# State sums of the S5 stage: from VectorE to GpSimd, in a hybrid decoder step on one core

## The chip, the core and the metric

The kernel runs on one core of one Trainium2 chip. The core has a matrix engine (TensorE, PE in the rows; its weight loads are PEld), a vector engine (VectorE, DVE), a scalar engine (ScalarE, ACT), GpSimd (POOL) and SyncE (SP, which issues most transfers here). They share an on-chip memory, SBUF; matrix products land in PSUM, called ps in the rows. Each engine runs its own list of instructions in order, and semaphores make one engine wait for another. The metric is the device time of one execution in microseconds (us), lower is better.

## What is computed

One inference step of a two-layer decoder, for a prompt of 256 positions and for 8 sequences with 4 new tokens each. Layer 0 is attention and gated linear attention, layer 1 an S5 state-space layer; a squared-ReLU channel mixer and a per-layer embedding follow each. The change lies in the S5 layer:

```python
    # 64 groups, one complex 64-dim state per group, u is the normed input
    bur = jnp.einsum('blgc,gpc->lbgp', u, bbr)
    bui = jnp.einsum('blgc,gpc->lbgp', u, bbi)
    ...
    _, _, xr, xi = lax.associative_scan(s5_combine, (ar, ai, bur, bui), axis=0)   # x[t] = lambda x[t-1] + bu[t]
    y = einsum(xr, c_re) - einsum(xi, c_im)      # y = Re(C x)
    y = y + d * n;  g = gelu(y);  zg = g @ w_glu
```

## The kernel before

The prompt is cut into 64 steps of four tokens, and the recurrence runs over the steps. The state indices lie on the 128 partitions in 32 blocks; the stage takes them in eight rounds of four blocks, numbered i from 0 to 7. A complex recurrence is made real by turning: the inputs v are multiplied by the cosines and sines of the angle of lambda to the power of the step (`rcos`, `rsin`), a real first-order scan with the magnitude (`mag`) runs over the steps, and its result is turned back by the same angles into the states X. The parts of a round are small functions in the list of VectorE:

- `turned_inputs(i)` (L2540, L2541): four products of the inputs, read from PSUM, with `rcos` and `rsin`, 128x256 each.
- `turning_back(i)` (L2562): two products of 128x512, from the scan's result `zs` into `pq` (two tiles in `sq`, used by every round).
- `turned_sums(i)` (L2547, L2548): a sum and a difference of 128x256 that finish the turned inputs.
- `states(i)` (L2568, L2569): a difference and a sum of 128x252 (four blocks of 63 steps) from `pq` into X. The second raises the semaphore `turned_back`.
- `scanned(i)` (L2556): two scans of 128x256, real and imaginary. Ahead of them VectorE waits for `x_start`, which the second of the turned sums raises.
- `normed_inputs(i + 3)` (L2528): one product that empties a PSUM bank of inputs for a later round.

VectorE's loop runs over nine rounds: `turned_inputs(i)`, `turning_back(i - 1)`, `turned_sums(i)`, `states(i - 1)`, `scanned(i)`, `normed_inputs(i + 3)`. The ninth has only `turning_back(7)` and `states(7)`. Behind the loop come `lo_half` (L2594, 128x1024) and `n_lo` (L1971, 128x288), which make the low parts of the first weights and inputs of the gated projection w_glu; its first half needs `lo_half(0, 0)` and four `n_lo`, the other four `n_lo` wait for ScalarE.

TensorE in each round makes the inputs of round i + 3 (L1427, L1363) and then `outputs(i)`: eight products with a Toeplitz matrix (L1435), in rounds 5 to 7 three products that only keep it busy (L1405), then a wait for `turned_back` at i + 1, and 16 products of X with C (L1443, L1444). Behind `outputs(7)` the products of the gated projection (L883 to L885) begin. ScalarE copies last states, applies GELU to the outputs (L1880) and makes the high parts of weights.

GpSimd makes `rcos`, `rsin` and `mag` ahead of the stage (tensor operations recorded at the helper's line L786), issues one transfer (L821), and then waits for `states_ready`, which VectorE raises after the stage, to issue two transfers of final states and one of the next embedding (L823 to L825).

Of the kernel before, what the change touches and what calls it, by code (L numbers as in the profile page):

```python
# [16 lines left out]
ALU = mybir.AluOpType  # L17
# [22 lines left out]
JP = TP // TS  # L40
# [235 lines left out]
def program(nc, ins, outs):  # L276
    g = plan()
    ctx = ExitStack()
    with ctx:
# [5 lines left out]
        with ExitStack() as names:  # L285
            inside, used = ([("a2hi", FB * T)] + [(f"hi{i}", UNIT) for i in range(HI[3])] + [("nhi", DB * T), ("phi", 2 * T), ("up1_lo", DB * T)]), S5A["Bre"][0]
            assert used == 0
            used = sum(size for _, size in inside)
            inside += [("between", S5A["a2"][0] - used), ("a2lo", FB * T)]
            assert inside[-2][1] > 0  # L290
            split = {n: names.enter_context(nc.sbuf_tensor(f"{n}_split", [P, size], F32R)) for n, size in shared[:-1] + inside}
        with ExitStack() as names:
            inside = [("before", sum(size for _, size in shared[:-1]) + AB["temp"][0])] + [(f"in_hi{i}", UNIT) for i in range(HI[0])] + [("in_nhi", DB * T)]
            assert HI[0] * UNIT <= AB["temp"][1]
            for n, size in inside:
                split[n] = names.enter_context(nc.sbuf_tensor(f"{n}_split", [P, size], F32R))
        with ExitStack() as names:

            inside = [("to_c", sum(size for _, size in shared[:-1]) + S5A["Cre"][0])] + [(f"up_hi{i}", UNIT) for i in range(HI[1])] + [("up_nhi", DB * T), ("up_lo", DB * T)]
            used = S5A["Cre"][0] + HI[1] * UNIT + 2 * DB * T  # L300
            assert used <= S5A["toep"][0]
            inside += [("to_a2", S5A["a2"][0] - used)] + [(f"a2{part}{half}", HALF) for half in range(2) for part in ("hi", "lo")]
            assert 4 * HALF == FB * T and UNIT <= HALF
            for n, size in inside:
                split[n] = names.enter_context(nc.sbuf_tensor(f"{n}_split", [P, size], F32R))
# [32 lines left out]
        def view(buf, offset, size, **shape):  # L338
            v = buf[:, offset:offset + size]
            if shape:  # L340
                keys = list(shape)
                v = v.rearrange("p (" + " ".join(keys) + ") -> p " + " ".join(keys), **{k: shape[k] for k in keys})
            return v
# [167 lines left out]
        to = a20 + SB * J  # L511
# [7 lines left out]
        X = view(arena, b0, 2 * SB * 128, r=2, s=SB, j=128)  # L519
# [7 lines left out]
        pq = [view(sq, 512 * i, 512, r=2, s=4, j=JP) for i in range(2)]  # L527
# [96 lines left out]
        def blocks_of(i, j=None):  # L624

            at = 16 * (i // 4) + i % 4
            return slice(at, at + 13, 4) if j is None else slice(at + 8 * j, at + 8 * j + 5, 4)
# [65 lines left out]
        def _(pool):  # L693
# [125 lines left out]
            pool.memset(mag[:, :, 0:1], 0.0).then_inc(rotation_ready, 1)  # L819
            pool.wait_ge(main_ready, g.of[("proj", 0, 7)][2])  # L820
            pool.dma_start(pT[:, 0:512], ins["x0"]).then_inc(x0_in, 16)  # L821
            pool.wait_ge(states_ready, 1)
            pool.dma_start(outs["s5_p"], arena[:, fin0:fin0 + 64]).then_inc(out_done, 16)  # L823
            pool.dma_start(outs["s5_s"], arena[:, vs0:vs0 + 512]).then_inc(out_done, 16)
# [1116 lines left out]
        def _(dve):  # L1941
            step = [0]
            V = nc.vector
# [581 lines left out]
            def normed_inputs(i):  # L2525

                ps = result(dve, ("u", i))
                V.tensor_tensor(ustk[:, blocks_of(i)], ps[:, 0:4 * J].rearrange("p (b j) -> p b j", j=J), bc(rsi.unsqueeze(1), [P, 4, J]),  # L2528
                                ALU.mult).then_inc(bank_of(("u", i)), 1)

            def turned_inputs(i):

                if i:
                    dve.wait_ge(scan_ready, 2 * i)
                for j in range(2):
                    name = ("v5", 2 * i + j)
                    ps = result(dve, name)
                    two = slice(2 * j, 2 * j + 2)
                    v = ps[:, 0:4 * J].rearrange("p (s r j) -> p r s j", s=2, r=2)[:, :, :, 0:JP]
                    V.tensor_tensor(z[:, :, two], v, bc(rcos[:, blocks_of(i, j)].unsqueeze(1), [P, 2, 2, JP]), ALU.mult).then_inc(bank_of(name), 1)  # L2540
                    V.tensor_tensor(zt[:, :, two], v, bc(rsin[:, blocks_of(i, j)].unsqueeze(1), [P, 2, 2, JP]), ALU.mult).then_inc(bank_of(name), 1)  # L2541

            def turned_sums(i):

                for j in range(2):
                    copied(dve, ("v5", 2 * i + j))
                V.tensor_tensor(z[:, 0], z[:, 0], zt[:, 1], ALU.add).then_inc(x_start, 1)  # L2547
                V.tensor_tensor(z[:, 1], z[:, 1], zt[:, 0], ALU.subtract).then_inc(x_start, 1)  # L2548

            def scanned(i):  # L2550

                if i >= 2:
                    dve.wait_ge(wfin_ready, i - 1)
                dve.wait_ge(x_start, 2 * i + 2)
                for r in range(2):
                    V.tensor_tensor_scan(flat(zs[i % 2][:, r]), flat(mag[:, 4 * i:4 * i + 4]), flat(z[:, r]), 0.0, ALU.mult, ALU.add).then_inc(scan_ready, 1)  # L2556

            def turning_back(i):

                dve.wait_ge(scan_ready, 2 * i + 2)  # L2560
                for x, rot in zip(pq, (rcos, rsin)):
                    V.tensor_tensor(x, zs[i % 2], bc(rot[:, blocks_of(i)].unsqueeze(1), [P, 2, 4, JP]), ALU.mult).then_inc(pow_done, 1)  # L2562

            def states(i):

                dve.wait_ge(pow_done, 2 * i + 2)
                to = X[:, :, blocks_of(i), 1:JP]
                V.tensor_tensor(to[:, 0], pq[0][:, 0, :, 0:JP - 1], pq[1][:, 1, :, 0:JP - 1], ALU.subtract).then_inc(x_ready, 1)  # L2568
                V.tensor_tensor(to[:, 1], pq[0][:, 1, :, 0:JP - 1], pq[1][:, 0, :, 0:JP - 1], ALU.add).then_inc(turned_back, 1)  # L2569

            copied(dve, ("ss", 3))
            for i in range(3):
# [2 lines left out]
            for i in range(9):  # L2575
                if i < 8:
                    turned_inputs(i)
                if i:
                    turning_back(i - 1)
                if i < 8:  # L2580
                    turned_sums(i)
                if i:
                    states(i - 1)
                if i < 8:
                    scanned(i)
                if i + 3 < 8:
                    normed_inputs(i + 3)
# [225 lines left out]
```

## Time and profile before

| | us |
|---|---|
| median of 3 runs | 987.06 (984.12 to 991.71) |
| the profiled execution's own time | 988.64 |
| its span, first to last instruction | 987.0 |
| TensorE busy (share of the span) | 943.7 (96%) |
| VectorE busy | 631.8 (64%) |
| ScalarE busy | 473.6 (48%) |
| GpSimd busy | 127.6 (13%) |

The profile is of one execution. Busy time is the union of an engine's instructions; a row of a timeline gives the start, the duration, the engine, the line, the operation and its tiles (out<-in), and in square brackets how long the engine sat idle before and what released it. Consecutive instructions of one line stand in one row with their number (x2). VectorE's next instruction often starts a little before the last one ends, so the distance of starts is what an instruction costs its queue. The S5 loop lies between 642 and 690 us of the span.

### The profile page before, as it was taken

Reading aid. Unit: us, or ns where it says so; the run is one execution under the profiler, and the core shown is the slowest. Engines: PE = TensorE matmul, PEld = TensorE weight load, DVE = VectorE, ACT = ScalarE, POOL = GpSimd, SP = SyncE. Lnnn points to the kernel's source line nnn. Section 1 sums busy time; section 2 is a strip of 40 time slices with the busy share of each in tenths; the row PEclk is TensorE's granted clock in tenths of the full one; section 3 lists DMA queues with packets and bytes.
Section 4 is the critical chain, followed back from the end, with each engine's and each line's share of the span. In section 5 each row is a group of like instructions: output and inputs, shape, how many; then the busy total and the mean of one; then the engine's idle time right before and its main releaser. Section 6 shows DMA issues by size and latency. Waiting matters only on the chain.

```text
span 987.0 us, 17733 instructions
## 1 busy us (share of the span) xinstructions
PE 943.7 (96%) x6831; PEld 868.3 (88%) x6831; DVE 631.8 (64%) x1118; ACT 473.6 (48%) x834; POOL 127.6 (13%) x215
## 2 busy tenths in 40 slices
PE   6999999989999799999999979999999999999997
PEld 6998478779888489999999967778999999999997
DVE  5653897788687258975586564399766666443453
ACT  6433565554334145755343546336665655433353
POOL 3420141000013220000000318800000000000000
PEclk9999999999879899999999999999999999999999
DMA  8580033211327653444444420500444444444431
GB/s 321 199 313 22 22 93 85 87 53 55 107 92 209 252 188 136 171 171 171 160 155 160 167 86 1 208 18 1 153 171 159 158 157 168 165 154 153 155 143 48
DMA packets 34773, 135.42 MB, mean 137 GB/s; under 512 B 5273, under 2 KB 17817, under 8 KB 22146
## 3 DMA queue, kind: packets, MB, share of 16 engines
q1 hardware_dynamic: 28802, 117.76, 33.3%
q0 software_dynamic: 5888, 16.53, 4.9%
q8 instruction: 54, 0.88, 0.4%
q14 instruction: 29, 0.24, 0.1%
HBM read 130.11 MB, written 4.17 MB: 136 GB/s over the span
## 4 chain that ended last, share of the span: by engine, by line
PE 77%; DVE 13%; ACT 3%; issue 3%; DMA 3%; SPq 1%; DVEq 0%; ACTq 0%; POOLq 0%
PE ps L883 18%; PE ps L884 17%; PE ps L885 17%; PE ps L915 4%; PE ps L1088 2%; PE ps L1090 2%; PE ps L1089 2%; DMA ring<-in_stream 2%; DVE arena L2411 1%; PE ps L1011 1%; PE ps L1427 1%; PE ps L1204 1%; DVE arena L2156 1%; DVE const L2556 1%; DVE arena L2152 1%
## 5 line engine op out<-in xcount | busy, mean ns | idle before, releaser
L885 PE MATMUL ps<-a2hi_split,ring_split 128*128 128x288 f32 x512 | 150.5, 294 | 0.0
L885 PEld LDWEIGHTS ps<-a2hi_split,ring_split 128*128 128x128 f32 x512 | 96.4, 188 | 0.0
L883 PE MATMUL ps<-nhi_split,hi_split 128*128 128x288 f32 x320 | 95.1, 297 | 0.1
L885 PE MATMUL ps<-nhi_split,ring_split 128*128 128x288 f32 x320 | 94.1, 294 | 0.0
L1967 DVE TENSOR_TENSOR ring_split<-ring,hi_split 128x2048 fp32r<-128x2048 f32 x36 | 82.2, 2285 | 17.5 <-ACT hi_split L1539 17.5
L1539 ACT ACTIVATE hi_split<-ring 128x2048 fp32r<-128x2048 f32 x36 | 68.7, 1910 | 31.4 <-PE ps L885 22.7
L1088 PE MATMUL ps<-sq_split,hT_split 128*128 128x288 f32 (+1 forms) x256 | 80.1, 313 | 3.6 <-DVE pages_lo_split L2134 3.3
L883 PE MATMUL ps<-up_nhi_split,up_hi_split 128*128 128x288 f32 x256 | 76.2, 298 | 0.9 <-DVE arena L2350 0.9
L1089 PE MATMUL ps<-wuk_lo_split,hT_split 128*128 128x288 f32 (+1 forms) x256 | 76.6, 299 | 0.0
L1090 PE MATMUL ps<-sq_split,pages_lo_split 128*128 128x288 f32 (+1 forms) x256 | 76.5, 299 | 0.0
L1539 ACT ACTIVATE up_hi_split<-ring 128x2048 fp32r<-128x2048 f32 x28 | 53.6, 1913 | 46.5 <-PE ps L885 44.8
L883 PE MATMUL ps<-a2hi_split,hi_split 128*128 128x288 f32 x256 | 75.8, 296 | 0.0
L884 PE MATMUL ps<-up_lo_split,hi_split 128*128 128x288 f32 x256 | 75.5, 295 | 0.0
L884 PE MATMUL ps<-up_lo_split,up_hi_split 128*128 128x288 f32 x256 | 75.5, 295 | 0.0
L884 PE MATMUL ps<-a2lo_split,hi_split 128*128 128x288 f32 x256 | 75.5, 295 | 0.0
L885 PE MATMUL ps<-up_nhi_split,ring_split 128*128 128x288 f32 x256 | 75.3, 294 | 0.0
L1967 DVE TENSOR_TENSOR ring_split<-ring,up_hi_split 128x2048 fp32r<-128x2048 f32 x28 | 63.9, 2284 | 11.7 <-ACT up_hi_split L1539 11.7
L915 PE MATMUL ps<-nT,ring 128*128 128x288 f32 x256 | 64.3, 407 | 0.0
L883 PEld LDWEIGHTS ps<-nhi_split,hi_split 128*128 128x128 f32 x320 | 60.0, 187 | 0.4 <-issue 0.3
L885 PEld LDWEIGHTS ps<-nhi_split,ring_split 128*128 128x128 f32 x320 | 60.2, 188 | 0.0
L915 PEld LDWEIGHTS ps<-nT,ring 128*128 128x128 f32 x256 | 48.3, 190 | 13.5 <-issue 0.4
L1088 PEld LDWEIGHTS ps<-sq_split,hT_split 128*128 128x128 f32 x256 | 51.2, 200 | 6.7 <-DVE pages_lo_split L2134 3.5
(426 smaller groups left out, 2597.5 us busy)
## 6 DMA issues: line engine op xcount, KB each, us to landing
ring<-in_stream SPq DMA_DIRECT2D x96, 1024.0 KB, 4.8
arena<-in_ckvT SPq DMA_DIRECT2D x64, 128.0 KB, 2.1
arena<-in_ckv POOLq DMA_DIRECT2D x23, 128.0 KB, 3.1
ring<-in_ckv POOLq DMA_DIRECT2D x21, 128.0 KB, 2.4
arena<-in_ckv SPq DMA_DIRECT2D x20, 128.0 KB, 2.8
arena<-in_wu POOLq DMA_DIRECT2D x1, 2240.0 KB, 10.2
arena<-in_s POOLq DMA_DIRECT2D x4, 512.0 KB, 3.5
out_gla_s<-arena POOLq DMA_DIRECT2D x4, 512.0 KB, 2.9
```

The costliest lines, as they stand in the source:

```text
L883: pe.matmul(ps[:, 0:T], wh[:, k, col:col + P], xh, start=first and k == which[0], stop=False)
L884: pe.matmul(ps[:, 0:T], wh[:, k, col:col + P], xl, start=False, stop=False)
L885: mm = pe.matmul(ps[:, 0:T], wl[:, k, col:col + P], xh, start=False, stop=last and k == which[-1])
L915: mm = pe.matmul(ps[base:base + m, 0:T], wv[:, k, col:col + m], rhs(k), start=first and k == which[0], stop=last and k == which[-1])
L1011: mm = pe.matmul(ps[0:NOPE, 0:T], wuk[:, k, key_columns(h):key_columns(h) + NOPE], ckvn[:, k], start=k == 0, stop=k == KB - 1)
L1088: pe.matmul(out, hi, wuk_hi[:, k, cols], start=start, stop=False, skip_group_check=True)
L1089: pe.matmul(out, hi, wuk_lo[:, k, cols], start=False, stop=False, skip_group_check=True)
L1090: return pe.matmul(out, lo, wuk_hi[:, k, cols], start=False, stop=stop, skip_group_check=True)
L1204: pe.matmul(ps[:, lo:lo + TS], s0[h % 2][:, b], qb[:, h, lo:lo + TS], start=False, stop=False, skip_group_check=True)
L1427: mm = pe.matmul(ps[:, (2 * n + r) * J:(2 * n + r) * J + J], bm[:, blk].rearrange("p i c -> p (i c)"), ustk[:, blk], start=n == 0 and r == ...
L1539: act.activation(hi_part(v)[:, :], ring[SPLITS[v] % RING][:, :], ACT.Copy).then_inc(hi_ready, 1)
L1967: V.tensor_tensor(lo_parts[slot][:, :], ring[slot][:, :], as_whole(hi_part(v)[:, :]), ALU.subtract).then_inc(unit_split, 1)
```

## The change

`states(i)` leaves VectorE's list and goes to GpSimd's, behind the transfer at L821 (the same lines are L827 and L828 in the kernel after, whose later lines are numbered 10 higher or, behind the loop, 4 higher). GpSimd waits for both products of `turning_back(i)`, then makes the difference and the sum. As `pq` is used by every round, `turning_back(i)` on VectorE now waits until the sums of round i - 1 are done.

```diff
@@ -819,6 +819,16 @@
             pool.memset(mag[:, :, 0:1], 0.0).then_inc(rotation_ready, 1)
             pool.wait_ge(main_ready, g.of[("proj", 0, 7)][2])
             pool.dma_start(pT[:, 0:512], ins["x0"]).then_inc(x0_in, 16)
+
+            def states(i):
+
+                pool.wait_ge(pow_done, 2 * i + 2)
+                to = X[:, :, blocks_of(i), 1:JP]
+                pool.tensor_tensor(to[:, 0], pq[0][:, 0, :, 0:JP - 1], pq[1][:, 1, :, 0:JP - 1], ALU.subtract).then_inc(x_ready, 1)
+                pool.tensor_tensor(to[:, 1], pq[0][:, 1, :, 0:JP - 1], pq[1][:, 0, :, 0:JP - 1], ALU.add).then_inc(turned_back, 1)
+
+            for i in range(8):
+                states(i)
             pool.wait_ge(states_ready, 1)
             pool.dma_start(outs["s5_p"], arena[:, fin0:fin0 + 64]).then_inc(out_done, 16)
             pool.dma_start(outs["s5_s"], arena[:, vs0:vs0 + 512]).then_inc(out_done, 16)
@@ -2557,16 +2567,12 @@
 
             def turning_back(i):
 
+                if i:
+                    dve.wait_ge(x_ready, i)
+                    dve.wait_ge(turned_back, i)
                 dve.wait_ge(scan_ready, 2 * i + 2)
                 for x, rot in zip(pq, (rcos, rsin)):
                     V.tensor_tensor(x, zs[i % 2], bc(rot[:, blocks_of(i)].unsqueeze(1), [P, 2, 4, JP]), ALU.mult).then_inc(pow_done, 1)
-
-            def states(i):
-
-                dve.wait_ge(pow_done, 2 * i + 2)
-                to = X[:, :, blocks_of(i), 1:JP]
-                V.tensor_tensor(to[:, 0], pq[0][:, 0, :, 0:JP - 1], pq[1][:, 1, :, 0:JP - 1], ALU.subtract).then_inc(x_ready, 1)
-                V.tensor_tensor(to[:, 1], pq[0][:, 1, :, 0:JP - 1], pq[1][:, 0, :, 0:JP - 1], ALU.add).then_inc(turned_back, 1)
 
             copied(dve, ("ss", 3))
             for i in range(3):
@@ -2579,8 +2585,6 @@
                     turning_back(i - 1)
                 if i < 8:
                     turned_sums(i)
-                if i:
-                    states(i - 1)
                 if i < 8:
                     scanned(i)
                 if i + 3 < 8:
```

On VectorE, one round of the loop before, from the last of the turned inputs to the next round's normed inputs (const, tmp, sq and arena are SBUF, ps is PSUM):

```order
L2541 TENSOR_TENSOR tmp<-ps,arena 128x2x128
L2562 TENSOR_TENSOR sq<-const,arena 128x512 x2
L2547 TENSOR_TENSOR const<-const,tmp 128x256
L2548 TENSOR_TENSOR const<-const,tmp 128x256
L2568 TENSOR_TENSOR arena<-sq 128x4x63
L2569 TENSOR_TENSOR arena<-sq 128x4x63
L2556 SCALAR_TENSOR_TENSOR const<-arena,const 128x256 x2
L2528 TENSOR_TENSOR arena<-ps,rs 128x4x72
```

The same place now:

```order
L2551 TENSOR_TENSOR tmp<-ps,arena 128x2x128
L2575 TENSOR_TENSOR sq<-const,arena 128x512 x2
L2557 TENSOR_TENSOR const<-const,tmp 128x256
L2558 TENSOR_TENSOR const<-const,tmp 128x256
L2566 SCALAR_TENSOR_TENSOR const<-arena,const 128x256 x2
L2538 TENSOR_TENSOR arena<-ps,rs 128x4x72
```

The two sums are gone, and the scans stand right behind the turned sums whose end they wait for.

On VectorE at the end of the loop before, from the last scans to the low parts of the gated projection:

```order
L2556 SCALAR_TENSOR_TENSOR const<-arena,const 128x256 x2
L2562 TENSOR_TENSOR sq<-const,arena 128x512 x2
L2568 TENSOR_TENSOR arena<-sq 128x4x63
L2569 TENSOR_TENSOR arena<-sq 128x4x63
L2594 TENSOR_TENSOR ring_split<-ring,glu_hi_split 128x1024
L1971 TENSOR_TENSOR nT_split<-nT,glu_nhi_split 128x288 x4
```

The same place now:

```order
L2566 SCALAR_TENSOR_TENSOR const<-arena,const 128x256 x2
L2575 TENSOR_TENSOR sq<-const,arena 128x512 x2
L2598 TENSOR_TENSOR ring_split<-ring,glu_hi_split 128x1024
L1981 TENSOR_TENSOR nT_split<-nT,glu_nhi_split 128x288 x4
L2598 TENSOR_TENSOR ring_split<-ring,glu_hi_split 128x1024
```

The low parts follow the last products of turning back at once; the last states are GpSimd's, at the same time.

## Rows read from the trace of the kernel before

**Rows 1.** Chain that ended last, in the S5 loop: start, us, what.
```profile
650.92 0.41 DVE arena L2569
...
682.82 0.42 DVE arena L2569
```

**Rows 2.** Busy time by stretch: us, busy of each engine, granted clock, DMA.
```profile
650.00:660.00 10.00, 8.41 (x79) 7.26 (x79) 10.00 (x26) 4.06 (x13) 0.00 (x0) 1.00 0.00 0
690.00:700.00 10.00, 10.00 (x77) 10.00 (x76) 7.91 (x13) 8.91 (x13) 0.00 (x0) 1.00 0.30 103
```

**Rows 3.** Timeline of VectorE, one round of the loop: start us, us, engine, line.
```profile
664.89 1.28 DVE L2562 TENSOR_TENSOR sq<-const,arena 128x512 f32<-128x512 f32 x2
666.10 0.42 DVE L2547 TENSOR_TENSOR const<-const,tmp 128x256 f32<-128x256 f32 x1
666.43 0.42 DVE L2548 TENSOR_TENSOR const<-const,tmp 128x256 f32<-128x256 f32 x1
666.77 0.41 DVE L2568 TENSOR_TENSOR arena<-sq 128x252 f32<-128x252 f32 x1
667.10 0.41 DVE L2569 TENSOR_TENSOR arena<-sq 128x252 f32<-128x252 f32 x1
667.43 1.26 DVE L2556 TENSOR_TENSOR_SCAN const<-arena,const 128x256 f32<-128x256 f32 x2
668.61 0.43 DVE L2528 TENSOR_TENSOR arena<-ps,rs 128x288 f32<-128x288 f32 x1
668.96 0.41 DVE L2540 TENSOR_TENSOR const<-ps,arena 128x256 f32<-128x256 f32 x1
```

**Rows 4.** Timeline of VectorE in round 0, where no sums of states stand between.
```profile
645.40 0.42 DVE L2548 TENSOR_TENSOR const<-const,tmp 128x256 f32<-128x256 f32 x1
645.86 1.27 DVE L2556 TENSOR_TENSOR_SCAN const<-arena,const 128x256 f32<-128x256 f32 x2
```

**Rows 5.** Timeline of GpSimd ahead of the loop, single operations on SBUF.
```profile
609.70 0.97 POOL L786 TENSOR_TENSOR arena<-arena 128x256 f32<-128x256 f32 x1
...
611.46 0.63 POOL L786 TENSOR_TENSOR arena<-arena 128x256 f32<-128x256 f32 x1
...
612.17 0.74 POOL L786 TENSOR_TENSOR arena<-arena 128x256 f32<-128x256 f32 x1
...
618.45 1.06 POOL L786 TENSOR_TENSOR arena<-arena 128x512 f32<-128x512 f32 x1
...
620.72 1.27 POOL L786 TENSOR_TENSOR arena<-arena 128x512 f32<-128x512 f32 x1
```

**Rows 6.** Timeline of VectorE at the same times.
```profile
609.64 0.46 DVE L2383 TENSOR_TENSOR hT<-hT,tmp 128x288 f32<-128x288 f32 x1
...
618.66 0.46 DVE L2378 TENSOR_TENSOR tmp<-ps,rs 128x288 f32<-128x288 f32 x1 [3.09 <-PE ps L915]
...
621.14 1.18 DVE L2383 TENSOR_TENSOR hT<-hT,tmp 128x288 f32<-128x288 f32 x1
```

**Rows 7.** Timeline of VectorE at the loop's end.
```profile
684.45 1.29 DVE L2562 TENSOR_TENSOR sq<-const,arena 128x512 f32<-128x512 f32 x2
...
686.12 0.41 DVE L2569 TENSOR_TENSOR arena<-sq 128x252 f32<-128x252 f32 x1
686.45 1.22 DVE L2594 TENSOR_TENSOR ring_split<-ring,glu_hi_split 128x1024 fp32r<-128x1024 f32 x1
687.58 1.56 DVE L1971 TENSOR_TENSOR nT_split<-nT,glu_nhi_split 128x288 fp32r<-128x288 f32 x4
689.06 1.22 DVE L2594 TENSOR_TENSOR ring_split<-ring,glu_hi_split 128x1024 fp32r<-128x1024 f32 x1
```

**Rows 8.** Timeline of TensorE at the loop's end, outputs of rounds 6 and 7.
```profile
683.38 0.41 PE L1443 MATMUL ps<-arena 128*128 128x71 f32 x2 [0.79 <-DVE arena L2569]
...
686.09 1.67 PE L1405 MATMUL ps<-hT,const 128*128 128x288 f32 x6
687.59 0.34 PE L1443 MATMUL ps<-arena 128*128 128x71 f32 x2
```

## Prediction

> **What bounds the kernel now.** I read the shares of busy time first: TensorE 96% of the span. A stage off TensorE can therefore matter only where TensorE waits for it. The chain that ended last shows one such place: between 650.92 and 683.24 us it runs through VectorE [rows 1], with the second state sum of each round in it. The busy time by stretch agrees: from 650 to 660 VectorE is busy for 10.00 of 10 us and TensorE for 8.41, at a granted clock of 1.00; from 690 on TensorE is busy for 10.00 of 10 again [rows 2]. So the S5 loop is VectorE's, what follows is TensorE's, and a shift of the loop's last outputs passes to the end of the kernel one for one. The timeline of VectorE then gives the round: products of turning back at 664.89, turned sums at 666.10 and 666.43, state sums at 666.77 and 667.10, scans at 667.43, normed inputs at 668.61, turned inputs from 668.96 [rows 3].
>
> **What is taken from VectorE.** The two sums cost its queue 667.43 - 666.77 = 0.66 us a round [rows 3]. Not all of it comes back. The scans wait for the end of the turned sums; before, the state sums lay in that wait. In round 0, where none lie there, the scan starts 0.46 after the second turned sum (645.40 to 645.86) [rows 4], against a distance of 0.33 between the two turned sums [rows 3]. That is 0.13 of new wait. The saving is 0.66 - 0.13 = 0.53 us a round.
>
> **What GpSimd pays.** Its row nearest in size is 128x256, 0.63 us for one kind and 0.74 for the one that writes in pieces [rows 5]; the sums also write in pieces (four of 63), so I take 0.74. Bounds: 0.6, and 1.0 since no row has this four-dimensional form. Between two such operations lie 612.17 - 611.46 - 0.63 = 0.08 us [rows 5]. A pair alone is 0.74 + 0.08 + 0.74 = 1.56 us. From the products' end to the next products VectorE has some 4 us of other work, so the new wait ahead of `turning_back` should cost nothing: its cover is the turned sums, scans, normed and turned inputs. Without that cover the pair would cost 1.56 x 7 = 11 us. GpSimd has nothing queued behind the sums but three transfers that wait for the end of the stage anyway.
>
> **What the two engines do to each other.** Here the trace speaks against the change. VectorE's hT<-hT,tmp takes 0.46 us at 609.64, but 1.18 at 621.14, where a GpSimd operation runs from 620.72 to 621.99 [rows 5, 6]. It was held for 0.72 and so began in earnest at 621.86, 0.13 before GpSimd's end. The other way round, GpSimd's operation at 609.70 started 0.06 after VectorE's and took 0.97 instead of 0.74 [rows 5, 6]: it was held for 0.23, that is until 609.93, 0.29 after VectorE's start. An operation of VectorE that reads PSUM and one SBUF tile (tmp<-ps,rs at 618.66) takes 0.46 beside a GpSimd operation that takes a plain 1.06 [rows 5, 6]. So where VectorE reads two SBUF tiles and GpSimd reads SBUF, one waits for most of the other; with an operand in PSUM it doesn't. In the loop, the turned sums, the scans and the products of turning back have two SBUF inputs, as the low parts behind it do; turned and normed inputs read PSUM.
>
> The Trainium skill says this as a rule (page "SBUF — State Buffer", section "Who interferes with whom"): a VectorE instruction with two SBUF inputs and a GpSimd instruction that reads SBUF exclude each other for the whole instruction, and the one that starts first goes first. The rows agree on who is held, but the hold is 0.29 of VectorE's 0.46 and all but 0.13 of GpSimd's. With whole instructions, the two delays worked out below would each be 0.13 longer, 0.26 x 7 = 1.8 us more in all. Without the rule the sum would be that of the second rival.
>
> Now one round, with time 0 where the first turned sum starts. The products end at 0.07 (664.89 + 1.28 against 666.10) [rows 3]; TensorE follows a VectorE semaphore after 0.14 (683.24 to 683.38) [rows 1, 8], so GpSimd's difference asks at 0.21. The turned sum holds the port for 0.29 x 256 / 288 = 0.26. If GpSimd gets in there, it holds from 0.26 to 0.87 (0.74 - 0.13 = 0.61), and the second turned sum, due at 0.33, waits **0.54**. It runs from 0.87 and lets go at 1.13; GpSimd's sum, ready at 0.87 + 0.13 + 0.08 = 1.08, holds from 1.13 to 1.74. The scan, due 0.46 after the second turned sum at 1.33, waits **0.41**. The states are done at 1.87. Delay 0.95, saving 0.53: **a round is 0.42 us longer**. Seven rounds of sums (0 to 6) lie ahead of the last products: +2.9 us.
>
> **The loop's end.** Before, the last products let go of the queue at 684.45 + 1.21 = 685.66 [rows 3, 7]; now at 688.6. There `lo_half` of 1024 columns follows at once [rows 7], holding the port for 0.29 x 1024 / 288 = 1.03. GpSimd's last difference waits for it, holds from 1.03 to 1.64, one `n_lo` of 288 columns slips in until 1.93, the sum holds until 2.54 and ends at 2.67, and TensorE's last outputs start 0.14 later: 688.6 + 2.8 = 691.4. Before, they start at 687.59 [rows 8]. That is **+3.8 us**. TensorE's fillers in front (686.09 [rows 8]) are then done; the low parts of the gated projection are ready by then or shift with the outputs.
>
> The profiled execution took 988.64 (span 987.0 and 1.6 around it), so the sum gives 988.64 + 3.8 = 992.4. This execution lies 1.58 above the median of the three runs, 987.06; for a median I forecast 987.06 + 3.8 = **990.9 us**.
>
> **Rivals.**
> (1) GpSimd doesn't get in between two pipelined VectorE operations, only where VectorE pauses or reads PSUM. No row shows two such operations in a row beside a waiting GpSimd one. Then the difference gets in at 0.59, ahead of the scan's wait, and delays it to 1.20 instead of 0.79 (0.41); the sum waits until the scans are over. A round is 0.53 - 0.41 = 0.12 shorter, seven give -0.8. But at the end it waits for `lo_half`, four `n_lo` and `lo_half` again: 689.06 - 686.45 + 1.03 = 3.64 [rows 7], then 1.56 and 0.14: 684.8 + 5.34 = 690.1, or +2.6 on TensorE: 989.7.
> (2) The other side: GpSimd runs beside VectorE (the scans, which no row shows beside GpSimd, don't use the port, or the sums seldom meet it). VectorE gains 0.53 x 7 = 3.7. TensorE gains less: its outputs of round 7 follow those of round 6 by its own work (683.38 to 687.59 [rows 8]), and those of round 6 come 6 x 0.53 = 3.2 earlier less 0.36, as states would be done 0.14 + 1.56 = 1.70 after the products' end against 667.51 - 666.17 = 1.34 now [rows 3]. So -2.8: 984.3. It decides once the two delays are below 0.53 a round. Held operations at 609.70 and 621.14 speak against it.
> (3) Slower by over 1%: GpSimd's operations are much longer in this form. Sixteen of them (14 delays, two at the end) pass their extra time on, so another 6.1 us on top of 3.8 needs 0.38 each, 1.12 instead of 0.74; at 1.0 the result is +8.0. Nothing in the rows of 256 columns comes near it unheld.
>
> **How the numbers follow.** Forecast 0.50, rival 1 0.20, rival 2 0.17, rival 3 0.05; 0.08 for cases between (0.6 us an operation gives 3.8 - 16 x 0.14 = +1.6; 1.0 gives +8.0). A run of this kernel can't tell less than about 1% (9.9 us) from no change, and the three runs differ by 7.6. The range goes from 984.0, which takes in half of rival 2, to 994.5, which takes in operations of 0.97 us and leaves rival 3 out; what is left out is 0.08 + 0.05 and some 0.07 of the cases between. Faster by over 1% needs more than the loop's whole share of the sums (8 x 0.66 = 5.3): 0.01. Slower by over 1% is rival 3: 0.05. Same: 0.94.
>
> **What would show it.** Right: in the loop, one turned sum and one scan a round with some 0.9 us instead of 0.4 and 1.0 instead of 0.65, both GpSimd operations near 0.75 to 1.0, no idle time of VectorE ahead of `turning_back`, rounds of 5.8 us against 5.4. Rival 1: GpSimd operations of over 1 us in the trace, the second ending behind the scans. Rival 2: rounds of 4.9 and both engines at their plain durations. Wrong altogether: VectorE waiting for GpSimd ahead of the products, or outputs of round 7 that are not the thing TensorE waits for.

## Result and profile after

| | before | after |
|---|---|---|
| median (lowest to highest), four runs each | 985.77 (984.12 to 991.71) | 1007.11 (1000.53 to 1017.09) |
| ratio, with its 95% interval | | 1.0133 (1.0077 to 1.0188) |
| the profiled execution | 988.64 | 1005.83 |
| its span | 987.0 | 1004.2 |
| its mean granted clock of TensorE | 0.982 | 0.962 |
| first scan to gated projection (the loop) | 43.43 | 56.43 |

The change makes the kernel slower, by 7.6 to 18.5 us as the interval has it (0.0077 and 0.0188 times 985.77); the medians, of four runs each that lie up to 17 us apart, differ by 21.3. The forecast was 990.9, with 0.05 for slower by over 1%. Runs over 1.5% above the fastest of their kernel are left out of every ratio; in two of the experiments (e3, e5) the profiled run, whose trace shows the effect found below, is one of them, so their ratios say less than their traces.

The spans differ by 17.2 us, in three parts. From the start to the first scan it is 645.86 before and 650.07 after, +4.2: this arises in stages whose instructions the change doesn't touch (between 260 and 280 us the granted clock was 0.64 before and 0.50 after), and the first scan of the experiments below, with the same work ahead of it, starts anywhere from 642.47 to 661.32. From the first scan to the first product of the gated projection it is 43.43 and 56.43, **+13.0**. What follows takes 297.7 in both. So the loop alone is to be explained, and its length, first scan to gated projection, is the measure used below.

The page after: busy time and share of the span, number of instructions; then the granted clock over 40 slices.

```profile
PE 960.9 (96%) x6831; PEld 884.7 (88%) x6831; DVE 632.5 (63%) x1102; ACT 473.3 (47%) x834; POOL 140.3 (14%) x231
...
PEclk9999999989589899999999999976999999999999
```

VectorE's busy time is what it was (632.5 against 631.8), since what it saved it now spends held up; GpSimd has 12.7 us more. TensorE is busy for 17 us longer with as many products. The reason is in the second line: two slices, the 27th and 28th (some 650 to 700 us), have a clock of 7 and 6 tenths.

First VectorE, from the timeline after (its lines have numbers 10 higher in the loop, 4 higher behind it):

```profile
658.72 1.28 DVE L2575 TENSOR_TENSOR sq<-const,arena 128x512 f32<-128x512 f32 x2
659.92 0.42 DVE L2557 TENSOR_TENSOR const<-const,tmp 128x256 f32<-128x256 f32 x1
660.26 0.94 DVE L2558 TENSOR_TENSOR const<-const,tmp 128x256 f32<-128x256 f32 x1
661.30 1.60 DVE L2566 TENSOR_TENSOR_SCAN const<-arena,const 128x256 f32<-128x256 f32 x2
662.83 0.43 DVE L2538 TENSOR_TENSOR arena<-ps,rs 128x288 f32<-128x288 f32 x1
...
664.50 1.28 DVE L2575 TENSOR_TENSOR sq<-const,arena 128x512 f32<-128x512 f32 x2
...
685.85 0.43 DVE L2557 TENSOR_TENSOR const<-const,tmp 128x256 f32<-128x256 f32 x1 [2.88 <-ACT arena L1873]
...
695.72 0.42 DVE L2557 TENSOR_TENSOR const<-const,tmp 128x256 f32<-128x256 f32 x1 [5.08 <-ACT arena L1873]
...
702.11 1.22 DVE L2598 TENSOR_TENSOR ring_split<-ring,glu_hi_split 128x1024 fp32r<-128x1024 f32 x1 [2.83 <-ACT glu_hi_split L1549]
```

and GpSimd, same view:

```profile
660.08 0.83 POOL L827 TENSOR_TENSOR arena<-sq 128x252 f32<-128x252 f32 x1 [4.09 <-DVE sq L2575]
660.88 0.90 POOL L828 TENSOR_TENSOR arena<-sq 128x252 f32<-128x252 f32 x1
...
683.05 0.72 POOL L827 TENSOR_TENSOR arena<-sq 128x252 f32<-128x252 f32 x1 [3.87 <-DVE sq L2575]
683.73 0.72 POOL L828 TENSOR_TENSOR arena<-sq 128x252 f32<-128x252 f32 x1
```

Up to 682 us this is the round that was forecast. Against [rows 3], the second turned sum takes 0.94 instead of 0.42 and the pair of scans 1.60 instead of 1.26; GpSimd's sums take 0.83 and 0.90 beside them, and 0.72 where VectorE sits idle (683.05). A round is 664.50 - 658.72 = 5.78 us; before it is 5.39 (scans at 662.04 and 667.43). What was not forecast is the last three rows of VectorE: waits of 2.88, 5.08 and 2.83 us for ScalarE, in a loop where VectorE was to be the bound.

ScalarE waits for TensorE there (6.30 us ahead of its GELU, twice). TensorE's timeline tells why, before (round 1, then the inputs that follow):

```profile
658.31 1.11 PE L1435 MATMUL ps<-arena 128*128 128x72 f32 x8 [1.59 <-DVE arena L2528]
...
661.05 1.95 PE L1427 MATMUL ps<-arena 128*128 128x72 f32 x16
```

and after (L1445 is L1435 before, L1437 is L1427, L1415 is L1405):

```profile
663.31 1.11 PE L1445 MATMUL ps<-arena 128*128 128x72 f32 x8 [2.13 <-DVE arena L2538]
...
666.46 3.62 PE L1437 MATMUL ps<-arena 128*128 128x72 f32 x16
669.87 1.91 PE L1445 MATMUL ps<-arena 128*128 128x72 f32 x8
...
674.99 3.62 PE L1437 MATMUL ps<-arena 128*128 128x72 f32 x16
...
693.76 2.93 PE L1415 MATMUL ps<-hT,const 128*128 128x288 f32 x6
...
706.50 0.38 PE L893 MATMUL ps<-glu_nhi_split,glu_hi_split 128*128 128x288 f32 x1
```

with busy time by stretch after (columns as in [rows 2], the granted clock is the third from the end):

```profile
650.00:660.00 10.00, 10.00 (x94) 8.35 (x94) 9.93 (x22) 1.93 (x9) 1.69 (x2) 1.00 0.01 2
660.00:670.00 10.00, 7.87 (x54) 7.26 (x54) 9.79 (x21) 4.70 (x14) 3.38 (x4) 0.78 0.01 2
670.00:680.00 10.00, 10.00 (x49) 10.00 (x49) 9.79 (x19) 2.58 (x11) 3.46 (x4) 0.50 0.00 0
680.00:690.00 10.00, 10.00 (x49) 10.00 (x48) 6.95 (x17) 2.14 (x8) 1.39 (x2) 0.50 0.00 0
690.00:700.00 10.00, 10.00 (x53) 9.07 (x53) 3.97 (x8) 4.93 (x16) 2.03 (x3) 0.68 0.01 2
```

In round 1 TensorE waits for VectorE's normed inputs, 2.13 us instead of 1.59. In the outputs behind the wait, at about 665.6, its clock falls from 1.00 to 0.50, that is from 2.4 to 1.2 GHz, and stays there until about 696 us although TensorE is busy for 10.00 of 10. The 16 products of the inputs take 3.62 us instead of 1.95. A round of TensorE now takes 674.99 - 666.46 = 8.53 us, more than VectorE's 5.78, so TensorE is the bound, then ScalarE's GELU is late, and then VectorE. The clock comes back at about 696, as the first three fillers end (L1415, 288 columns; each leaves two records, so the row has x6).

### The profile page after: what moved, and what is told of

Its sections match the earlier page's. It is cut to its first block, busy times and chain, and to the rows that moved or that the text cites. A ratio compares the mean times of both kernels' runs of the same rounds, so it can differ in the third digit from the quotient of the medians.

```text
span 1004.2 us, 17740 instructions
## 1 busy us (share of the span) xinstructions
PE 960.9 (96%) x6831; PEld 884.7 (88%) x6831; DVE 632.5 (63%) x1102; ACT 473.3 (47%) x834; POOL 140.3 (14%) x231
## 4 chain that ended last, share of the span: by engine, by line
PE 78%; DVE 10%; POOL 4%; issue 3%; ACT 2%; DMA 2%; SPq 1%; DVEq 0%; POOLq 0%; ACTq 0%
PE ps L893 18%; PE ps L895 18%; PE ps L894 18%; POOL arena L786 4%; PE ps L925 3%; PE ps L1098 2%; PE ps L1100 2%; PE ps L1099 2%; DMA ring<-in_stream 1%; PE ps L1437 1%; PE ps L1445 1%; PE ps L1454 1%; PE ps L1453 1%; PE ps L1021 1%; PE ps L1229 1%
```

## Experiments

The reading to test: of the 13.0 us, some 4 are the longer rounds and the end, as forecast, and some 9 are TensorE's clock, which a longer wait of TensorE brings down. The rivals: GpSimd's work as such is the cause, or TensorE slows down for a reason that has nothing to do with its waits.

| | loop, us | ratio to before (95%) | median (lowest to highest, runs) |
|---|---|---|---|
| before | 43.43 | | |
| after | 56.43 | 1.0133 (1.0077 to 1.0188) | 1007.11 (1000.53 to 1017.09, 4) |
| e1, longer rounds without GpSimd | 56.63 | 1.0152 (1.0113 to 1.0191) | 1003.02 (998.78 to 1006.83, 4) |
| e6, only two longer rounds | 56.64 | 1.0161 (1.0115 to 1.0207) | 1008.17 (1006.21 to 1017.35, 5) |
| e2, after with fillers | 47.92 | 1.0043 (1.0003 to 1.0082) | 995.36 (989.76 to 1000.16, 8) |
| e3, after with fillers in round 1 only | 56.13 | 1.0049 (1.0011 to 1.0088) | 997.22 (990.03 to 1010.95, 10) |
| e8, before with fillers | 43.45 | 0.9982 (0.9945 to 1.0019) | 990.82 (985.01 to 1004.85, 12) |
| e4, sums behind the scans, fillers | 45.49 | 1.0052 (1.0017 to 1.0087) | 993.59 (989.71 to 1000.10, 10) |
| e5, sums behind the scans, no fillers | 60.12 | 0.9991 (0.9959 to 1.0024) | 992.85 (984.23 to 1011.97, 12) |
| e7, as e4 with fewer fillers | 43.39 | 0.9996 (0.9962 to 1.0029) | 991.53 (985.69 to 994.28, 12) |
| e9, as e7 with one filler at the end | 40.98 | 0.9997 (0.9965 to 1.0029) | 990.51 (986.28 to 999.37, 12) |
| e10, as e7 with none at the end | 40.97 | 0.9990 (0.9957 to 1.0023) | 990.30 (987.72 to 997.97, 12) |

The loop's length is that of the one profiled execution; ratio and median are those of the whole kernel, the ratio against runs of the kernel before made beside it. Some expectations count the loop from the first inputs made on TensorE instead, which gives 48.05 before.

**e1 and e6: longer rounds without GpSimd.** The kernel before, with two additional sums on VectorE (0.49 us a round) ahead of `states(i)`, in rounds 0 to 6 (e1) or 0 and 1 alone (e6). They write scratch.

```diff
             def states(i):

                 dve.wait_ge(pow_done, 2 * i + 2)
+                if i < 7:            # e6: if i < 2
+                    dve.wait_ge(dve_step, step[0])
+                    step[0] += 2
+                    V.tensor_tensor(rs[:, J:T], sq[:, 0:T - J], sq[:, 512:512 + T - J], ALU.add).then_inc(dve_step, 1)
+                    V.tensor_tensor(sq[:, 1024:1152], sq[:, 0:128], sq[:, 512:640], ALU.add).then_inc(dve_step, 1)
```

> The kernel before, with two more additions on VectorE (216 and 128 columns into unused scratch) ahead of the state sums of rounds 0 to 6: some 0.29 + 0.20 = 0.49 us a round, about what the change cost VectorE (0.39 to 0.42), and nothing on GpSimd. Theory 1 (the loss is TensorE's clock: longer VectorE rounds make TensorE wait over 2 us for the inputs' bank in round 1, and the granted clock then goes to 0.50): the wait before the Toeplitz products of round 1 grows from 1.59 to over 2.1 us, the clock falls to 0.50 behind it, and the time is 12 to 16 us above before. Theory 2 (the loss comes of GpSimd and VectorE sharing a port): only 7 x 0.49 = 3.4 us above before, clock 1.00.

TensorE in e1, then one of its stretches (670 to 680 has 0.50 as well):

```profile
655.92 1.11 PE L1435 MATMUL ps<-arena 128*128 128x72 f32 x8 [2.25 <-DVE arena L2528]
...
659.26 3.62 PE L1427 MATMUL ps<-arena 128*128 128x72 f32 x16
```

```profile
660.00:670.00 10.00, 10.00 (x49) 10.00 (x48) 10.00 (x25) 3.65 (x14) 0.00 (x0) 0.50 0.00 0
```

The round is 5.89 (products of turning back at 651.22 and 657.11), GpSimd does nothing (0.00), and the loop is 13.2 us longer: a wait of 2.25 against 2.13, the same fall of the clock, the same loss. GpSimd as such isn't the cause.

> The kernel before with the two added VectorE operations in the sums of rounds 0 and 1 alone (about 1.0 us in all), so that TensorE has its one long wait ahead of the Toeplitz products of round 1 (about 2.2 us) and rounds of 5.4 us behind it, as before. If that one wait decides the clock: it falls to 0.50 behind it and the time is 8 to 15 us above before. If it takes the waits of many rounds: the clock stays at 1.00 and the time is 0.5 to 1.5 us above before.

```profile
674.77 1.11 PE L1435 MATMUL ps<-arena 128*128 128x72 f32 x8 [1.89 <-DVE arena L2528]
```

```profile
670.00:680.00 10.00, 8.11 (x63) 7.50 (x61) 10.00 (x25) 5.59 (x16) 0.00 (x0) 0.85 0.01 2
680.00:690.00 10.00, 10.00 (x49) 10.00 (x48) 9.15 (x24) 2.79 (x12) 0.00 (x0) 0.50 0.00 0
```

The wait in round 1 is 1.89 us, less than the 2.2 expected, and the clock falls all the same. The extra 1.0 us of VectorE costs 13.2 of the loop. Rounds of 5.78 (after), 5.89 (e1) and 5.39 from the third on (e6) end in the same 56.4 to 56.6 us: once the clock has fallen, VectorE's round no longer matters. e1 and e6 change nothing in TensorE's list, only how long it waits; so a longer wait in round 1 is enough.

**e2 and e3: the change with TensorE kept busy.** The kernel after, with filler products of 128x288 (about 0.5 us each at full clock) ahead of the inputs, where TensorE would otherwise wait. e2 also has five fillers instead of three in rounds 5 to 7.

```diff
                 if i + 3 < 8:
+                    if i in {1: 4, 2: 2, 3: 2, 4: 2}:      # e3: {1: 4}
+                        keep_busy(bank(("v5", 2 * i + 6))[:, 0:T], {1: 4, 2: 2, 3: 2, 4: 2}[i])
                     inputs(i + 3, 0)
...
-                    keep_busy(bank(("y5", i + 1) if i < 7 else ("glu_a", 0))[:, 0:T], 3)
+                    keep_busy(bank(("y5", i + 1) if i < 7 else ("glu_a", 0))[:, 0:T], 5)   # e2 alone
```

> The changed kernel with filler products on TensorE: four ahead of the inputs made in round 1 (about 2 us), two in rounds 2 to 4, five instead of three in rounds 5 to 7. Theory 1: no wait of TensorE over 1.2 us is left, the clock stays at 1.00 through the loop, VectorE's rounds stay 5.8 us as in the changed kernel, and the time is 3 to 6 us above before, so 9 or more below the changed kernel. Theory 2: as slow as the changed kernel, 12 us or more above before.

Stretches of e2, and TensorE at its loop's end:

```profile
660.00:670.00 10.00, 9.79 (x75) 8.44 (x74) 9.79 (x21) 5.04 (x16) 3.00 (x4) 1.00 0.01 2
670.00:680.00 10.00, 9.87 (x85) 9.52 (x83) 9.90 (x20) 3.63 (x14) 2.10 (x3) 1.00 0.00 0
680.00:690.00 10.00, 10.00 (x76) 9.27 (x75) 9.72 (x19) 5.38 (x17) 3.40 (x4) 1.00 0.01 2
```

```profile
696.65 2.64 PE L1415 MATMUL ps<-hT,const 128*128 128x288 f32 x10
699.12 0.34 PE L1453 MATMUL ps<-arena 128*128 128x71 f32 x2
...
700.83 0.38 PE L893 MATMUL ps<-glu_nhi_split,glu_hi_split 128*128 128x288 f32 x1
```

and GpSimd there:

```profile
695.73 1.63 POOL L827 TENSOR_TENSOR arena<-sq 128x252 f32<-128x252 f32 x1 [2.64 <-DVE sq L2577]
697.33 0.93 POOL L828 TENSOR_TENSOR arena<-sq 128x252 f32<-128x252 f32 x1
```

The clock stays at 1.00 with VectorE's rounds as long as after (5.78), and the loop is 8.5 us shorter than after, 4.5 longer than before. Of the 4.5, some 0.7 are the experiment's own fillers: GpSimd's last sum ends at 697.33 + 0.93 = 698.26 and TensorE could follow at 698.40, but the fillers hold it until 699.12. Without them the loop would be about 3.8 us longer than before, which is the forecast's sum. So the split of the 13.0 is 3.8 to 4.5 for what was forecast and 8.5 to 9.2 for the clock. In whole times too, all eight runs of e2 (up to 1000.16) lie below all four of after (from 1000.53). The fillers do two things at once, though: they shorten the waits and give TensorE other products; e2 doesn't separate the two.

> The changed kernel with the four filler products of round 1 alone. Theory 1 in its narrow form (the one wait of 2.13 us is the cause): clock 1.00, 3 to 5 us above before. Theory 1 in its wide form (each round leaves about 1.2 us of waiting, and a later one brings the clock down as well): the clock falls in a later round, 6 to 12 us above before. Theory 2: as slow as the changed kernel.

TensorE in e3, then two stretches:

```profile
669.86 1.67 PE L1445 MATMUL ps<-arena 128*128 128x72 f32 x8 [0.91 <-DVE arena L2540]
```

```profile
660.00:670.00 10.00, 9.09 (x73) 7.99 (x73) 9.79 (x19) 5.25 (x15) 3.40 (x4) 1.00 0.01 2
670.00:680.00 10.00, 10.00 (x49) 10.00 (x50) 9.79 (x20) 2.89 (x12) 3.39 (x4) 0.51 0.00 0
```

Here the runs part: six of ten took 990.0 to 998.7 us, four 1003.0 to 1011.0. The profiled one is of the latter; its clock falls at about 670, after a wait of only 0.91 us in the next round. That is the wide form of the expectation; the median, of both kinds together, is 8.4 us above that of before. Filling the longest wait alone is thus not reliable. And the length of one wait doesn't decide: before, 1.59 us left the clock at 1.00.

**e8: the fillers alone.** The kernel before with three fillers in round 1 and one in round 2, for whether they speed up the kernel by themselves.

```diff
+                    if i in {1: 3, 2: 1}:
+                        keep_busy(bank(("v5", 2 * i + 6))[:, 0:T], {1: 3, 2: 1}[i])
```

> The kernel before with fillers on TensorE alone: three products ahead of the inputs made in round 1, one in round 2, in the place of its waits of 1.59 and 0.71 us. VectorE bounds the loop there, so by theory 1 nothing changes as long as the clock was held anyway: within 1 us of before, a loop of 48 us. If the waits of the kernel before now and then brought the clock down as well, the time comes out 1 to 4 us below before.

The waits are filled, the loop takes 43.45 against 43.43, and the kernels can't be told apart. What e2 wins is the clock's loss undone, and not a gain that fillers bring to the kernel before as well. Two of the twelve runs took 1003.7 and 1004.9 us: long runs occur with these waits filled too.

**e4 and e5: the sums behind the scans.** Is the other part, the 3.8 us, the meeting of the two engines? GpSimd waits for the next round's scans as well and so works while VectorE reads PSUM; the sums of the last two rounds stay on VectorE. e4 has e2's fillers in rounds 1 to 4, e5 has none. The diff is against the kernel after; the wait ahead of `turning_back` goes with it, for rounds 1 to 6 alone.

```diff
             def states(i):                      # GpSimd
                 pool.wait_ge(pow_done, 2 * i + 2)
+                pool.wait_ge(scan_ready, 2 * i + 4)
...
-            for i in range(8):
+            for i in range(6):
                 states(i)
...
+                if i > 6:                       # VectorE, behind turned_sums(i)
+                    states(i - 1)
```

> The changed kernel with GpSimd waiting for the scans of the next round before it makes the state sums, so that they lie beside VectorE's operations on PSUM; rounds 6 and 7 make their sums on VectorE as before; TensorE has the fillers of rounds 1 to 4 (four, two, two, two). If the port is what stretches the turned sums (0.94 against 0.42) and the scans (1.61 against 1.27), both are back at their plain times, GpSimd's operations at 0.72, and a round is 5.39 - 0.53 = 4.9 us. By theory 1 with the clock held: 1 to 3 us below before. If the clock falls again: 5 us or more above before.

VectorE, then GpSimd, in e4:

```profile
655.43 0.42 DVE L2561 TENSOR_TENSOR const<-const,tmp 128x256 f32<-128x256 f32 x1
655.95 1.27 DVE L2569 TENSOR_TENSOR_SCAN const<-arena,const 128x256 f32<-128x256 f32 x2
...
660.92 1.27 DVE L2569 TENSOR_TENSOR_SCAN const<-arena,const 128x256 f32<-128x256 f32 x2
```

```profile
657.37 0.72 POOL L828 TENSOR_TENSOR arena<-sq 128x252 f32<-128x252 f32 x1 [3.58 <-DVE const L2569]
658.05 0.72 POOL L829 TENSOR_TENSOR arena<-sq 128x252 f32<-128x252 f32 x1
```

The turned sum is back at 0.42, the scans at 1.27, GpSimd at 0.72, and a round takes 660.92 - 655.95 = 4.97 us, 0.42 less than before. So the longer round of the change is the meeting of the two engines. The kernel gains nothing from it, where 1 to 3 us below before was expected: TensorE with two fillers needs 5.44 us a round (inputs at 663.95 and 669.39), and the loop is 2.1 longer than before, with the clock at 1.00.

> As the run behind the scans, without any added filler products on TensorE. There TensorE's own list with the fillers took 5.44 us a round and had become the bound (VectorE waited for ScalarE, ScalarE for TensorE). Without them TensorE needs 4.5 us a round and VectorE 5.0. Theory 1 (only TensorE's clock and VectorE's rounds count): no wait of TensorE over 1.2 us, clock 1.00, the loop from the first inputs to the gated projection 45.5 to 47.5 us against 48.05 before, 0.5 to 2.5 us below before. Theory 2 (GpSimd in the loop costs by itself): a loop of 48 us or more, and not below before.

TensorE in e5, then its stretches:

```profile
654.99 0.41 PE L1454 MATMUL ps<-arena 128*128 128x71 f32 x2 [1.22 <-POOL arena L829]
```

```profile
650.00:660.00 10.00, 8.79 (x63) 8.03 (x59) 9.86 (x24) 4.18 (x13) 2.80 (x4) 0.79 0.01 2
660.00:670.00 10.00, 10.00 (x51) 8.95 (x50) 6.09 (x14) 2.46 (x11) 1.40 (x2) 0.50 0.01 2
```

As the sums come later, TensorE's first outputs wait 1.22 us for GpSimd, and in the profiled run the clock falls at about 656. The expectation, a loop of 45.5 to 47.5 from the first inputs with the clock at 1.00, is missed there. Of twelve runs four took 1001 us or more and eight 984 to 997: they part as in e3.

**e7, e9, e10: fillers matched to the gain.** As e4, with two fillers in rounds 0 and 1 and one in rounds 2 to 4 (e7); then one (e9) or none (e10) instead of three in rounds 5 to 7.

```diff
-                    if i in {1: 4, 2: 2, 3: 2, 4: 2}:
+                    if i in {0: 2, 1: 2, 2: 1, 3: 1, 4: 1}:
...
-                    keep_busy(bank(("y5", i + 1) if i < 7 else ("glu_a", 0))[:, 0:T], 3)
+                    keep_busy(bank(("y5", i + 1) if i < 7 else ("glu_a", 0))[:, 0:T], 1)   # e9; e10: left out
```

> As the run behind the scans, with the fillers on TensorE matched to VectorE's round of 5.0 us: two ahead of the inputs made in rounds 0 and 1, one in rounds 2 to 4 (0.5 us each). If the one thing missing there was TensorE's clock: no wait of TensorE of 1 us or more in the loop, clock 1.00, the loop 46.5 to 48 us against 48.05 before, and the time 0 to 2 us below before. If it needs the sums on VectorE for other reasons: a loop of over 48.5 us.

The clock holds, and the seventh scan starts 29.75 us after the first, against 32.13 before: 2.4 us gained. From the first inputs the loop takes 47.32, within the expectation, but in this trace those inputs came late, at a clock that was low ahead of them (0.58 from 640 to 644). From the first scan the loop ends where it did (43.39): from 677.60 on TensorE works through its list without a wait, with the three fillers a round that were there to cover waits which are now gone.

> As the matched run behind the scans, with one filler product instead of three in each of rounds 5 to 7. There TensorE had no wait from 677.6 us to the gated projection at 694.9, so the loop's end was its own list, fillers of 4.5 us among it. With 3 us of them gone VectorE is last: from the first scan to the gated projection 40.5 to 41.5 us against 43.4 both there and before, clock 1.00, and the time 1 to 3 us below before. If the clock falls in rounds 5 to 7: 5 us or more above before.

> As the run with one filler, with none in rounds 5 to 7. VectorE is last already, so no more is won: 40.5 to 41.5 us from the first scan to the gated projection if the clock holds. TensorE's waits grow by 0.5 us a round to about 1 us; if that brings the clock down, the time is 5 us or more above before.

TensorE in e9, behind the loop:

```profile
686.89 0.38 PE L894 MATMUL ps<-glu_nhi_split,glu_hi_split 128*128 128x288 f32 x1
...
690.91 0.37 PE L894 MATMUL ps<-glu_nhi_split,glu_hi_split 128*128 128x288 f32 x1 [0.58 <-DVE nT_split L1984]
```

With fewer fillers the loop is 2.4 us shorter than before in both traces, the clock at 1.00 and the waits at most 0.95 us. What follows the loop takes 298.6 us in both instead of 297.7, with a wait of 0.58 for the low parts that VectorE makes. The rest, some 1.5 us or 0.2%, is within the interval of either ratio (0.33% to each side): no version was measurably faster than the kernel before.

## Why the prediction was wrong

**What held.** With the clock at 1.00 (before, e2) the bound was read rightly: VectorE's round. The terms on VectorE came out closely:

| term | forecast | measured |
|---|---|---|
| second turned sum to scan, longer by | 0.54 | 1.04 - 0.46 = 0.58 |
| scan to normed inputs, longer by | 0.41 | 1.53 - 1.18 = 0.35 |
| a round, longer by | 0.42 | 5.78 - 5.39 = 0.39 |
| GpSimd's sum, unhindered | 0.74 | 0.72 |
| end of the loop, with the clock at 1.00 (e2) | 3.8 | 3.8, and 0.7 of fillers |

The two delays together are 0.93 of a forecast 0.95. The Trainium skill (page "SBUF — State Buffer", section "SBUF: two separate sides") says that of such a pair the instruction that starts first keeps the shared ports for its whole length and the other waits. By the prediction's estimate for whole instructions the delays would have been 1.21; the trace agrees on who is held, but the hold is shorter than the instruction.

**Rivals.** The first (GpSimd doesn't get in between two VectorE operations) falls: its difference runs at 660.08, between the two turned sums, and its sum ends at 661.78, within the scans. The second (no meeting) falls with the 0.94 of the turned sum; e4 shows what it would have been like, rounds of 4.97. The third, the only one that forecast slower, names another cause: it needs GpSimd operations of 1.12 us, and in the rounds they took 0.83 and 0.90. The result was in its direction, and not its mechanism.

**The step that failed** is in the first part: "So the S5 loop is VectorE's". It was read from the kernel before, 8.41 of 10 us of TensorE busy at a granted clock of 1.00 [rows 2], and carried over to the kernel after. The sum has VectorE's longer round (7 x 0.42) and the loop's end, and no term for TensorE's clock: that it stays at 1.00 when TensorE waits longer was taken for granted, without a reason. The runs showed in its place a clock that falls to 0.50 behind a wait of 2.13 us, a round of TensorE of 8.53 us against VectorE's 5.78, and 8.5 to 9.2 us for that of the loop's 13.0 (e2 against after). The rest of the prediction's sentence, that a shift of the last outputs passes to the end one for one, held: what follows the loop takes 297.7 us in both. One of the prediction's own signs of being wrong came true: behind 696 us TensorE has no wait left in the loop, so the outputs of round 7 aren't what it waits for.

The 1.59 us of that stretch in which TensorE isn't busy are one wait, in round 1, and by the forecast's own term it was to become 1.59 + 0.42 = 2.01; it became 2.13. That was the question to ask: what happens to the clock when TensorE stands still for so long? The trace of before shows falls, but doesn't settle it. TensorE ahead of the loop, and one stretch:

```profile
576.74 0.72 PE L864 MATMUL ps<-sq,ones 128*128 128x288 f32 x2 [2.55 <-DVE sq L1984]
589.92 3.49 PE L1338 MATMUL ps<-arena 128*32 128x128 f32 x64 [3.25 <-DVE tmp L2381]
635.49 1.66 PE L1363 MATMUL ps<-hT,const 128*32 128x288 f32 x24 [2.06 <-DVE arena L2506]
```

```profile
262.00:272.00 10.00, 10.00 (x46) 9.84 (x45) 4.12 (x8) 1.84 (x5) 1.06 (x2) 0.50 0.29 105
```

Behind the wait of 3.25 us the clock was 0.50 (590 to 593), and so it was behind those of 3.31 (ending at 217.89) and 5.37 (at 330.32). Behind 2.55 and 2.06 it was 1.00 (577 to 587, 636 to 646). From 262 to 272 it was 0.50 though TensorE had been busy for 9.80 of the 10 us ahead. So the trace gave reason to name a falling clock as a rival, and the code did too, with its fillers in rounds 5 to 7, products that only keep TensorE busy. Its waits of 2.06 and 2.55 us spoke for a clock that holds, and what chance the rival deserved would have been a guess; a run like e6 answers it. The rival would have had its place (round 1), its price (rounds at half clock of 8.53 us against 5.39) and its own sign. It was missing, and so the chance of slower was 0.05.

**What stays open.** Which pattern of work and waits brings the clock down. In round 1, waits of 1.89, 2.13 and 2.25 us (e6, after, e1) were followed by it in each of the three traces, and all 13 runs of these kernels were long (998.8 us or more; of all 90 runs of the kernel before four were). But the length of a wait doesn't decide alone. Ahead of the loop a wait of 2.06 us left the clock at 1.00 in after and e1 as well (639.76, 632.08), and the 2.55 us shown above left it at 1.00 in nine of the twelve traces and was followed by 0.50 in e3, e7 and e8. Smaller waits in the loop went both ways: 1.59 in round 1 left it at 1.00 (before), 0.95 in e10 too, but 1.22 in e5 and 0.91 in e3 were followed by the fall in the profiled run. Five of ten runs of e3 and eight of twelve of e5 took under 997 us, too short for the loop of the profiled run: with the earliest first scan of any trace (642.47), that loop, the 297.7 behind it and 1.6 around the span, e3 would take 998 and e5 1002 (an estimate). The runs don't tell what differs. A run's time alone doesn't tell either whether the clock fell in the loop, as the first scan starts up to 19 us apart; so for the few long runs of the kernel before, none of them profiled, it isn't known.

## What to carry to other kernels

A wait of TensorE isn't slack just because the granted clock reads 1.00 around it. Ask how much longer the change makes it, and look in the same trace for what the clock did behind such waits; where the trace goes both ways, as here, lengthen the wait by itself in a run (e6) before the forecast. Where the clock may fall, price it as TensorE's round at half clock, for as long as the stretch lasts, and cover the wait with filler products, no more than fit into it. Two engines that hold each other up can be set apart in time (here GpSimd behind the scans), but the gain counts only if the list of the next engine has room for it.

## What the runs showed of the hardware

- Once at 0.50, the clock stayed there for 30 us (666 to 696) with TensorE busy for 10.00 of every 10 us, in products of 72 columns. It came back as three filler products of 288 columns ended (from 693.76). One us more of VectorE's work, over two rounds, cost 13 us this way (e6).
- The same wait of TensorE at the same place, 2.55 us, left the clock at 1.00 in nine traces and was followed by 0.50 in three.
- At half clock the 16 products of 72 columns took 3.62 us against 1.95, a factor of 1.86.
- A GpSimd operation with inputs in SBUF gets in between two VectorE operations that stand back to back (the second then took 0.94 us instead of 0.42), and the scan, with two inputs in SBUF, takes part in this as the sums do (1.60 against 1.27).
